# A decoder block whose second MLP product is built from seven products: GpSimd adds the sums for pieces (6,0) and (6,1) ahead of those for (7,0) and (7,1)

## The chip, the cores and the metric

The kernel runs on one core of a Trainium2 chip. The metric is the device time of one execution in microseconds (us); lower is better. Every engine of the core runs its own queue of instructions in order, and engines wait for each other by semaphores.

## The reference: what is computed

One decoder layer on 512 tokens of width 1024, in float32. The part that the change touches is the MLP at the end:

```python
h = rms_norm(x, norm_ffn_pre[l])
f = jnp.square(jax.nn.relu(h @ w_ff1[l])) @ w_ff2[l]     # 1024 -> 4096 -> 1024
x = x + rms_norm(f, norm_ffn_post[l])
```

Before it stands a token mixer (a projection to ten parts, three branches, a gated merge, a projection back), which the change leaves as it is.

## The kernel before

**Float32 from two halves.** Each matrix of weights comes from memory in units of 128x1024 float32 (512 KB). ScalarE rounds a unit to `w_hi` (line 521, `ff_hi`), VectorE writes the rest as `w_lo` (line 765, `ff_lo`), and TensorE makes each product from three: hi by hi, hi by lo, lo by hi (lines 1147 to 1151). `w_hi` and `w_lo` are rings of four buffers, so the unit u is split once TensorE is through with unit u-4.

**The MLP in quarters.** The hidden width of 4096 is cut into four quarters of 1024 (`q`). A quarter is 22 units: 8 of `w_ff1` (24 matmuls each), and then 14 pieces of `w_ff2` (12 matmuls each). The second matmul is made from seven products of half-size blocks instead of eight, as in Strassen's and Winograd's schemes; piece (p,h) is half h of what product p takes from the weights. TensorE's order is

```python
PIECES = ((1, 0), (5, 0), (2, 0), (1, 1), (5, 1), (6, 0), (2, 1), (6, 1),
          (3, 0), (3, 1), (7, 0), (7, 1), (4, 0), (4, 1))
```

The products 6, 7, 4 and 3 are laid on top of an earlier product in the same PSUM bank (`ON_TOP_OF`: 6 on 1, 7 on 6, 4 on 7, 3 on 5). TensorE may start them only when VectorE has added the earlier one to the result (`add_product`, line 1080). For 7 and 4 both halves are used token tile by token tile, so (4,0) and (4,1) are both needed at the start.

**Sums of weights.** Products 5, 6, 4 and 7 need a sum of blocks. It is made by the DMA: GpSimd issues a transfer from memory that adds onto what lies in the buffer (line 505, `add_blocks`). In 5, 6 and 4 the sum grows: (5,h) is loaded by SP into slot 6+h (tile `glu`) and one block is added; when it has been split, a second block is added in place for (6,h); when that has been split, a third for (4,h). The sum for (7,h) is apart: SP loads a block into one of the six slots that the plain loads use in turn (tiles `raw`, `raw_v`, `raw_c`), and GpSimd adds one onto it. In each quarter there are eight such transfers, 32 in all.

**What the queues wait for.** GpSimd waits, for (5,h) and (7,h), for SP's load of the slot (`raw_loaded`), and for (6,h) and (4,h), for the split of the piece that lay in the slot (`w_lo_ready`): (6,0) for the split of (5,0), (6,1) for that of (5,1), (4,0) and (4,1) for those of (6,0) and (6,1). ScalarE waits for the sum (`raw_added`) before `w_hi`. VectorE's order among the pieces (lines 1103 to 1121): for each piece in TensorE's order it waits for the piece to be done, adds finished products, and then splits the piece four further on. So the `w_lo` of (6,0) and of (2,1) stands ahead of the two adds of product 1, on which product 6 waits; and the `w_lo` of (4,1) stands ahead of the first add of product 7, on which product 4 waits. SP (lines 388 to 404) loads the 512 KB units in order, each when the one that was last in its slot has been split.

Of the kernel before, what the change touches and what calls it, by code (L numbers as in the profile page):

```python
# [94 lines left out]
def piece_unit(q, n):  # L95
    return ff_unit(q, KT + n)
# [26 lines left out]
def is_loaded(u):  # L123
    return piece_of(u)[0] not in ADDED or piece_of(u)[0] in LOADED
# [6 lines left out]
def earlier_in_slot(u):  # L131
    return [v for v in range(U_FF, u) if FF_SLOT[v] == FF_SLOT[u]]


def ff_loads(u):
    before = U_FF // RAW if FF_SLOT[u] < RAW else 0
    return 16 * (before + sum(is_loaded(v) for v in earlier_in_slot(u)) + 1)
# [6 lines left out]
def source(u, added=False):  # L144

    q, k = divmod(u - U_FF, PER_QUARTER)
    product, h = piece_of(u)
    if product is None:
        return U_FF + 2 * KT * q + k
    k_half, n_half = (ADDED if added else LOADED)[product]  # L150
    return U_FF + 2 * KT * q + KT + CH * n_half + 2 * k_half + h
# [50 lines left out]
def build(nc, x_d, units_d, cols_d, rows_d, ws_d, bs_d, out_d):  # L202
    with ExitStack() as ctx:
# [210 lines left out]
        def _(pool):  # L414
# [80 lines left out]
            def add_blocks(q, products):  # L495
                for n, (product, h) in enumerate(PIECES):
                    if product not in products:
                        continue
                    u = piece_unit(q, n)
                    slot = FF_SLOT[u]  # L500
                    if is_loaded(u):
                        pool.wait_ge(raw_loaded[slot], ff_loads(u))
                    else:
                        pool.wait_ge(w_lo_ready, earlier_in_slot(u)[-1] + 1)
                    pool.dma_start(slots[slot], units_d[source(u, added=True)],
                                   accum_op=ALU.add).then_inc(raw_added[slot], 16)

            for q in range(QUARTERS):
                add_blocks(q, (5,))
                add_blocks(q, (7,))  # L510
                add_blocks(q, (6,))
                add_blocks(q, (4,))

            for n, c in enumerate(FINAL):
# [247 lines left out]
        def _(dve):  # L762
# [313 lines left out]
            def add_product(q, product, t):  # L1076

                _, bank, (m_half, n_half, sign) = PRODUCTS[product]
                y = by_token[:, 2 * m_half + t, half_of(n_half)]
                nc.vector.tensor_tensor(y, y, ps[:, bank + t, :],  # L1080
                                        ALU.add if sign > 0 else ALU.subtract).then_inc(mlp_sum, 1)
# [343 lines left out]
```

## Time and profile before

| | us |
|---|---|
| median of 3 runs | 999.98 (999.39 to 1000.72) |
| the profiled execution | 999.11 |
| its span in the trace | 997.4 |
| outside the span | 1.7 |

The span is what the views of the trace divide; the profiled execution is 0.87 us under the median. In a row of the timeline stand the start, the time taken, the engine, the line and the tiles; in brackets the idle time of the engine before it and who ended that. "issue" there means that the profile shows no instruction that ended the wait; the landing of a transfer can be behind it. The profile models the end of each matmul: 128x512 ones are shown 0.39 us long but start 0.23 us apart in a full row.

### The profile page before, as it was taken

What the parts mean: (1) busy time and instruction counts of PE and PEld (TensorE: products, weight loads), DVE (VectorE), ACT (ScalarE), POOL (GpSimd) and SP (SyncE); (2) the same over time, 40 slices, a digit from 0 to 9 for tenths busy, and PEclk for the clock granted to TensorE, in tenths of its full rate; (3) what the DMA queues carried; (4) which work ended last, traced back from release to release, by engine and by line L of the source; (5) the groups of instructions that cost most, each with busy time, mean ns of one, the idle gap of its engine ahead of it and who ended that gap; (6) DMA issues with size and microseconds to landing.
All of it is one profiled execution on the core that took longest, in us unless ns stands there. A gap on an engine that the chain in (4) does not pass through costs nothing.

```text
span 997.4 us, 12346 instructions
## 1 busy us (share of the span) xinstructions
PE 969.9 (97%) x4380; PEld 805.7 (81%) x4380; DVE 675.3 (68%) x829; ACT 382.3 (38%) x493; POOL 98.3 (10%) x115
## 2 busy tenths in 40 slices
PE   5999999999999999999999999999899899999996
PEld 4888888888888888888888888898788788878885
DVE  5348889888888988886584443755645574565568
ACT  5333332333333322224463322545335434533543
POOL 3000000000000011114000000121100100110012
PEclk9999999999999999999999999999999999999999
DMA  6323322223223122233226234074845667475472
GB/s 218 118 82 112 106 89 90 100 95 103 95 86 105 64 98 91 84 106 112 100 87 251 93 100 165 23 224 118 205 152 150 132 179 202 113 195 178 118 126 85
DMA packets 34629, 123.35 MB, mean 124 GB/s; under 512 B 4000, under 2 KB 4128, under 8 KB 34592
## 3 DMA queue, kind: packets, MB, share of 16 engines
q1 hardware_dynamic: 28368, 100.84, 29.6%
q0 software_dynamic: 5120, 17.83, 10.5%
q10 hardware_dynamic: 1104, 4.19, 1.1%
q8 instruction: 23, 0.38, 0.1%
q14 instruction: 14, 0.11, 0.0%
HBM read 120.75 MB, written 2.10 MB: 123 GB/s over the span
## 4 chain that ended last, share of the span: by engine, by line
PE 95%; DVE 2%; issue 1%; ACT 1%; DMA 1%; POOL 0%; DVEq 0%; POOLq 0%; ACTq 0%
PE ps L1147 30%; PE ps L1151 30%; PE ps L1149 30%; DVE w_lo L765 1%; PE ps L1190 1%; PE ps L1304 1%; PE ps L1305 1%; PE ps L1303 1%; DVE wide L1080 1%; DMA conf<-x_in 1%; PE ps L1253 0%; PE ps L1254 0%; DVE wide L1093 0%; PE ps L1252 0%; ACT w_hi L521 0%
## 5 line engine op out<-in xcount | busy, mean ns | idle before, releaser
L765 DVE TENSOR_TENSOR w_lo<-raw,w_hi 128x1024 fp32r<-128x1024 f32 x130 | 160.4, 1237 | 115.7 <-ACT w_hi L521 115.4
L1147 PE MATMUL ps<-a_hi,w_hi 128*128 128x512 f32 x576 | 225.4, 391 | 0.0
L1149 PE MATMUL ps<-a_lo,w_hi 128*128 128x512 f32 x576 | 224.2, 389 | 0.0
L1151 PE MATMUL ps<-a_hi,w_lo 128*128 128x512 f32 x576 | 224.1, 389 | 0.0
L521 ACT ACTIVATE w_hi<-raw 128x1024 fp32r<-128x1024 f32 x130 | 137.0, 1056 | 198.5 <-PE ps L1151 135.5
L842 DVE SCALAR_TENSOR_TENSOR conf<-glu,cols,conf (+1 forms) x240 | 186.9, 779 | 27.5 <-DVE conf L842 26.4
L1147 PE MATMUL ps<-b_hi,w_hi 128*128 128x512 f32 x360 | 140.2, 390 | 0.0
L1151 PE MATMUL ps<-b_hi,w_lo 128*128 128x512 f32 x360 | 140.1, 389 | 0.0
L1149 PE MATMUL ps<-b_lo,w_hi 128*128 128x512 f32 x360 | 140.0, 389 | 0.0
L1149 PEld LDWEIGHTS ps<-a_lo,w_hi 128*128 128x128 f32 x576 | 108.2, 188 | 22.7 <-issue 0.5
L1147 PEld LDWEIGHTS ps<-a_hi,w_hi 128*128 128x128 f32 x576 | 108.1, 188 | 22.6 <-DVE w_lo L765 0.2
L1151 PEld LDWEIGHTS ps<-a_hi,w_lo 128*128 128x128 f32 x576 | 108.1, 188 | 22.5
L1147 PE MATMUL ps<-w_hi,set_hi 128*128 128x512 f32 x224 | 89.1, 398 | 8.4 <-DVE wide L1080 8.4
L1149 PE MATMUL ps<-w_lo,set_hi 128*128 128x512 f32 x224 | 88.3, 394 | 0.0
L1151 PE MATMUL ps<-w_hi,set_lo 128*128 128x512 f32 x224 | 88.1, 393 | 0.0
L1147 PEld LDWEIGHTS ps<-b_hi,w_hi 128*128 128x128 f32 x360 | 67.6, 188 | 14.2 <-DVE b_lo L766 0.3
L1151 PEld LDWEIGHTS ps<-b_hi,w_lo 128*128 128x128 f32 x360 | 67.6, 188 | 14.1
L1149 PEld LDWEIGHTS ps<-b_lo,w_hi 128*128 128x128 f32 x360 | 67.6, 188 | 14.0
L1147 PEld LDWEIGHTS ps<-w_hi,set_hi 128*128 128x128 f32 x224 | 42.8, 191 | 19.2 <-DVE w_lo L765 9.8
L765 DVE TENSOR_TENSOR w_lo<-glu,w_hi 128x1024 fp32r<-128x1024 f32 x24 | 29.4, 1223 | 37.9 <-ACT w_hi L521 35.7
L1151 PEld LDWEIGHTS ps<-w_hi,set_lo 128*128 128x128 f32 x224 | 42.8, 191 | 9.2
L1149 PEld LDWEIGHTS ps<-w_lo,set_hi 128*128 128x128 f32 x224 | 42.9, 192 | 8.8
(154 smaller groups left out, 1170.3 us busy)
## 6 DMA issues: line engine op xcount, KB each, us to landing
raw<-units_in SPq DMA_DIRECT2D x134, 512.0 KB, 3.3
glu<-units_in POOLq DMA_DIRECT2D x24, 512.0 KB, 6.1
raw_v<-units_in SPq DMA_DIRECT2D x22, 512.0 KB, 4.3
raw_c<-units_in SPq DMA_DIRECT2D x20, 512.0 KB, 4.1
glu<-units_in SPq DMA_DIRECT2D x8, 512.0 KB, 5.3
conf<-x_in SPq DMA_DIRECT2D x4, 512.0 KB, 8.0
glu<-rows_in ACTq DMA_DIRECT2D x4, 512.0 KB, 10.7
conf<-x_in ACTq DMA_DIRECT2D x1, 2048.0 KB, 9.0
```

What stands on the lines that cost most here:

```text
L521: return nc.scalar.activation(dst, src, ACT.Copy, scale=scale)
L765: return nc.vector.tensor_tensor(dst, src, hi, ALU.subtract)
L842: nc.vector.scalar_tensor_tensor(out=conf[:, tile, :], in0=glu[:, tile, k:k + SEQ], scalar=cols[:, tile, COL_CONF + k:COL_CONF + k + 1], i ...
L1080: nc.vector.tensor_tensor(y, y, ps[:, bank + t, :], ALU.add if sign > 0 else ALU.subtract).then_inc(mlp_sum, 1)
L1147: nc.tensor.matmul(ps[:, bank, :], left_hi, right_hi, start=first, stop=False, skip_group_check=on_top)
L1149: nc.tensor.matmul(ps[:, bank, :], left_hi, right_lo, start=False, stop=False, skip_group_check=on_top)
L1151: return nc.tensor.matmul(ps[:, bank, :], left_lo, right_hi, start=False, stop=final, skip_group_check=on_top)
L1190: mm = nc.tensor.transpose(ps[:, banks + g, k * P:(k + 1) * P], by_token[:, c, at:at + P], ident[:, :])
L1303: nc.tensor.matmul(out, w_hi[:, u.ring, w], b_hi[:, k, tokens], start=k == 0, stop=False)
L1304: nc.tensor.matmul(out, w_hi[:, u.ring, w], b_lo[:, k, tokens], start=False, stop=False)
L1305: mm = nc.tensor.matmul(out, w_lo[:, u.ring, w], b_hi[:, k, tokens], start=False, stop=k == KT - 1)
```

## The change

In `add_blocks`' calling loop the order of two calls is exchanged. GpSimd's order in a quarter was 5, 7, 6, 4 and is 5, 6, 7, 4, with h = 0 and 1 of each. The same 32 transfers are issued, with the same waits; no other engine's queue changes.

```diff
             for q in range(QUARTERS):
                 add_blocks(q, (5,))
+                add_blocks(q, (6,))
                 add_blocks(q, (7,))
-                add_blocks(q, (6,))
                 add_blocks(q, (4,))
```

GpSimd's queue in the first quarter and at the start of the second. `glu` is the tile of the growing sums; those that wait for `raw_loaded6` and `raw_loaded7` are (5,0) and (5,1); those on `raw_v` and `raw` are (7,0) and (7,1); those that wait for `w_lo_ready` are of 6 and 4:

```order
 L505 DMA glu<-units_in 128x1024 [waits raw_loaded6]
 L505 DMA glu<-units_in 128x1024 [waits raw_loaded7]
+L505 DMA glu<-units_in 128x1024 [waits w_lo_ready] x2
 L505 DMA raw_v<-units_in 128x1024 [waits raw_loaded2]
 L505 DMA raw_v<-units_in 128x1024 [waits raw_loaded3]
-L505 DMA glu<-units_in 128x1024 [waits w_lo_ready] x4
+L505 DMA glu<-units_in 128x1024 [waits w_lo_ready] x2
 L505 DMA glu<-units_in 128x1024 [waits raw_loaded6]
```

Four transfers of the growing sums stood in a row behind the two of product 7; now the two for product 6 stand ahead of them, and the two for product 4 behind.

GpSimd's queue in the last quarter, up to the reduction that follows it:

```order
 L505 DMA glu<-units_in 128x1024 [waits raw_loaded7]
+L505 DMA glu<-units_in 128x1024 [waits w_lo_ready] x2
 L505 DMA raw_v<-units_in 128x1024 [waits raw_loaded2]
 L505 DMA raw_v<-units_in 128x1024 [waits raw_loaded3]
-L505 DMA glu<-units_in 128x1024 [waits w_lo_ready] x4
+L505 DMA glu<-units_in 128x1024 [waits w_lo_ready] x2
 L432 TENSOR_SCALAR meansq<-sumsq 128x1 [waits sumsq_ready]
```

The same exchange; the queue still ends with the two transfers for product 4.

## Rows read from the trace of the kernel before

**Rows 1.** The page: span, and the chain that ended last, by engine.
```profile
span 997.4 us, 12346 instructions
...
PE 95%; DVE 2%; issue 1%; ACT 1%; DMA 1%; POOL 0%; DVEq 0%; POOLq 0%; ACTq 0%
```

**Rows 2.** Timeline, start and us taken: matmuls after the idle stretches, one a quarter.
```profile
710.39 0.76 PE L1147 MATMUL ps<-w_hi,set_hi 128*128 128x512 f32 x1 [2.65 <-DVE wide L1080]
...
796.55 0.47 PE L1147 MATMUL ps<-w_hi,set_hi 128*128 128x512 f32 x1 [2.88 <-DVE wide L1080]
...
880.68 0.74 PE L1147 MATMUL ps<-w_hi,set_hi 128*128 128x512 f32 x1 [2.27 <-DVE wide L1080]
...
964.56 0.47 PE L1147 MATMUL ps<-w_hi,set_hi 128*128 128x512 f32 x1 [0.40 <-DVE wide L1080]
```

**Rows 3.** Stretches: us, busy time (x instructions) by engine, PE clock, DMA share, GB/s.
```profile
710.40:713.50 3.10, 3.10 (x8) 2.44 (x9) 2.87 (x5) 1.59 (x2) 0.86 (x1) 0.51 0.91 174
796.50:799.60 3.10, 3.05 (x14) 2.55 (x14) 2.80 (x4) 1.72 (x2) 0.78 (x1) 1.00 1.00 188
880.70:884.20 3.50, 3.50 (x9) 2.76 (x10) 2.85 (x5) 2.00 (x2) 0.86 (x1) 0.51 0.97 199
```

**Rows 4.** Timeline of VectorE, first quarter.
```profile
684.94 1.23 DVE L765 TENSOR_TENSOR w_lo<-glu,w_hi 128x1024 fp32r<-128x1024 f32 x1 [3.50 <-ACT w_hi L521]
...
701.60 1.22 DVE L765 TENSOR_TENSOR w_lo<-glu,w_hi 128x1024 fp32r<-128x1024 f32 x1
707.28 1.23 DVE L765 TENSOR_TENSOR w_lo<-glu,w_hi 128x1024 fp32r<-128x1024 f32 x1 [4.46 <-ACT w_hi L521]
708.43 1.22 DVE L765 TENSOR_TENSOR w_lo<-raw_c,w_hi 128x1024 fp32r<-128x1024 f32 x1
709.56 1.27 DVE L1080 TENSOR_TENSOR wide<-wide,ps 128x512 f32<-128x512 f32 x2
```

**Rows 5.** Timeline of ScalarE, first quarter: splits of (6,0), (6,1), (4,0), (4,1).
```profile
706.12 1.06 ACT L521 ACTIVATE w_hi<-glu 128x1024 fp32r<-128x1024 f32 x1 [4.74 <-issue]
...
709.98 1.06 ACT L521 ACTIVATE w_hi<-glu 128x1024 fp32r<-128x1024 f32 x1 [1.85 <-issue]
...
723.07 1.06 ACT L521 ACTIVATE w_hi<-glu 128x1024 fp32r<-128x1024 f32 x1 [1.66 <-PE ps L1151]
725.79 1.06 ACT L521 ACTIVATE w_hi<-glu 128x1024 fp32r<-128x1024 f32 x1 [1.66 <-PE ps L1151]
```

**Rows 6.** Timeline of GpSimd: issues for (7,0), (7,1), (6,0), (6,1), (4,0).
```profile
685.08 0.86 POOL L505 DMA_DIRECT2D raw_v<-units_in  x1 [14.55 <-DMA raw_v<-units_in]
695.87 0.86 POOL L505 DMA_DIRECT2D raw_v<-units_in  x1 [9.94 <-DMA raw_v<-units_in]
696.41 1.21 POOL L505 DMA_DIRECT2D glu<-units_in  x1
703.12 0.86 POOL L505 DMA_DIRECT2D glu<-units_in  x1 [5.50 <-DVE w_lo L765]
708.80 0.86 POOL L505 DMA_DIRECT2D glu<-units_in  x1 [4.83 <-DVE w_lo L765]
```

**Rows 7.** Line 505 in 695:704, 781:790, 866:874, 952:960: (7,1), (6,0), (6,1).
```profile
DMA to landing us min/median/max: 6.5/6.8/9.6
...
L505 POOL DMA_DIRECT2D glu<-units_in x2: 863/1040/1218, 782.4 to 789.1; - x2
...
DMA to landing us min/median/max: 5.3/7.1/9.8
...
L505 POOL DMA_DIRECT2D glu<-units_in x2: 863/1040/1218, 867.1 to 873.8; - x2
...
DMA to landing us min/median/max: 5.2/6.8/9.3
...
DMA to landing us min/median/max: 5.4/5.6/7.4
```

**Rows 8.** Timeline of SP's queue: the load behind (7,1) and the next one.
```profile
697.07 12.92 SPq L404 DMA_DIRECT2D raw_c<-units_in  x2
```

## Prediction, made before the changed kernel was timed

> **What bounds the kernel now.** The page comes first. TensorE's matmuls are 95% of the chain that ended last [rows 1], so only a stretch in which TensorE stands still, or runs slower, can be saved. The timeline of TensorE over the MLP has one such stretch in every quarter, always ahead of the first matmul of piece (6,0) [rows 2]. The idle time there is counted from the modelled end of the matmul before, which is shown 0.39 us long where the next may start after 0.23. So the start is late by the idle time + 0.39 - 0.23: 2.81, 3.04, 2.43 and 0.56 us, together 8.84 us. Behind two of the four the granted clock is 0.51, the lower of its two levels, 1.2 GHz where full speed is 2.4: for 3.1 us after the first stall and 3.5 us after the third. Behind the second, the longest, it is 1.00 [rows 3]. A stretch of 3.1 us at 0.51 does the work of 1.6 us, so 1.5 us are lost, and 1.7 in the other: 3.2 us. Stalls and slow clock cost **12.1 us** in this execution.
>
> The reader should now follow one stall backwards, the first. TensorE was released at 710.39 by VectorE's add of product 1, which started at 709.56. That add stood in VectorE's order behind two splits, at 707.28 and 708.43, and the first of them, the `w_lo` of (6,0), had waited 4.46 us for ScalarE [rows 4]. ScalarE had been idle for 4.74 us and started the `w_hi` of (6,0) at 706.12, with no instruction that released it [rows 5]: what came was the sum. GpSimd had issued the transfer for (6,0) at 696.41, right behind that for (7,1) at 695.87 [rows 6], and it took 9.6 us to land, the largest of the three in that stretch [rows 7], so until 706.0. The same shape stands in the next two quarters (9.8 and 9.3 us), and a milder one in the last (7.4 us), which has a stall of 0.56 us only.
>
> When could it have been issued? The slot was free when the `w_lo` of (5,0) was done, at 684.94 + 1.23 = 686.2 [rows 4]. GpSimd stood until 695.87 at the wait for SP's load of (7,1) [rows 6], with (6,0) queued behind. This is what the exchange takes away: 10 us of waiting for another piece's load.
>
> **What the change takes away.** (6,0) is issued at 686.2 and lands some 6 us later, near 692. ScalarE needs it at about 701.5, so 9 us are to spare and the late sum is gone in all four quarters. What is late next at that place? VectorE's two splits then end by about 705.2 and the first add of product 1 by 705.8, before TensorE comes to (6,0) at 710.39 - 2.81 = 707.58. Its cover there is 1 us or more. So all 12.1 us go, if nothing new comes. Issuing costs GpSimd the same 0.86 us each in either order, and nobody waits for GpSimd itself there.
>
> **What the change adds.** The transfers move in GpSimd's queue past one wait. (6,1) may be issued only when (5,1) has been split, 701.60 + 1.22 = 702.8 [rows 4], and that moment is set by TensorE's pace, so its issue stays at 703.12 [rows 6]. (7,0) and (7,1), which used to go out at 685.08 and 695.87 in an emptier time, now stand behind it and go at about 703.7 and 704.2. (4,0), ready since the early split of (6,0) at about 704, goes at 704.8, and (4,1) when (6,1) has been split, near 711. **Five transfers in a row** replace a spread of them, and the last is the one to follow.
>
> The first of a row took 6.5, 5.3, 5.2 and 5.4 us [rows 7]; I take 5.4, so (6,1) lands at 708.5. The step from one landing to the next in such a row comes from the same rows, with issues 0.54 us apart for (7,1) and (6,0), and 6.7 us for (6,0) and (6,1) (703.12 - 696.41 [rows 6]; 782.4 to 789.1 and 867.1 to 873.8 [rows 7]).
> - With a plain load of SP's between them, as the one issued at 697.07 [rows 8]: 9.6 - 6.5 + 0.5 = 3.6, then 9.8 - 5.3 + 0.5 = 5.0 and 9.3 - 5.2 + 0.5 = 4.6. Mean 4.4 us.
> - Without one: 6.8 - 9.6 + 6.7 = 3.9, then 4.0 and 4.2. Mean 4.0 us. In the last quarter, where SP has no load left, 7.4 - 5.4 + 0.5 = 2.5 us.
>
> From (6,1) to (4,1) are four steps. SP issues loads when (2,1), (3,0) and (3,1) have been split, now near 705, 713.5 and 715, so three of the steps have a load between. They give 3 x 4.4 + 4.0 = 17.2 us, and (4,1) lands at 725.7. The bounds are 3 x 3.6 + 2.5 = 13.3 (721.8) and 3 x 5.0 + 4.2 = 19.2 (727.7). No row shows five in a queue, so both ends are kept; I take the means, as the busy quarters are the nearest.
>
> What does it meet? From the landing of a sum to TensorE's start behind the add, the first stall shows 0.1 us to ScalarE, 1.16 to VectorE's split, 1.15 to the next in its row and 0.83 from the start of the add to the matmul [rows 2, 4, 5], 3.2 us in all. The same order stands before product 4: split of (4,1), add of product 7, matmul. So TensorE starts (4,0) at 728.9. Without delay it would come there at 707.58 + 7 pieces x 2.72 (the step of 723.07 to 725.79 in [rows 5]) = 726.6. It is **2.3 us late**. In the kernel before, ScalarE took these two sums without waiting for them, released by TensorE [rows 5], so this stall is wholly new. (7,0) and (7,1) are wanted later in their turn (first matmul at 707.58 + 5 x 2.72 = 721.2) and land at about 713 and 717; (6,1) leaves 2 us of cover. These cost nothing, nor do SP's loads that come later, since the next quarter's units have 20 us and more.
>
> In the last quarter no load stands between: 959.6 + 5.4 + 4 x 2.5 = 975.0, and it is wanted by 964.0 + 19.0 - 3.2 = 979.8. It costs nothing, or 1.2 us at 4.0 us a step.
>
> **The sum.** Three new stalls of 2.3 us are 6.9 us. For the clock: the shortest old stall that it fell behind was 2.43 us and one of 3.04 us had none, so I charge one drop of 1.6 us for the three. Added: 8.5 us. Removed: 12.1 us. Net -3.6 us on 999.11 us gives 995.5 us, and on the median, which lies 0.87 us higher, **996.4 us**.
>
> A page speaks on the price of a transfer. The trace has 5.2 to 6.5 us for the first of a row of sums and steps of 2.5 to 5.0 us behind it [rows 7]. The Trainium skill ("DMA: Bandwidth & Descriptors", section "Anatomy of one DMA — SWDGE (gpsimd) path") fits a transfer issued by GpSimd as 2.0 us plus its bytes at 436 GB/s. By that, an estimate, 512 KB would take 3.2 us with steps of 1.2 us, the row of five would be over by about 713, and the time would be that of the first rival. The trace doesn't agree, at less than half the speed; these transfers add, which the fit doesn't treat.
>
> **The rivals.**
> - *The gain stays whole.* If the steps are short, 3.6 us or less with a load between, or if SP's loads fall behind the sums instead of between them (four steps of 3.9 us end at 724.1, half a microsecond or so late), (4,1) comes by 723.4 and nothing is late. For it: 2.5 us in the last quarter. Against it: all three busy quarters have 3.9 us or more where no load is between. Time: 999.98 - 12.1 = 987.9 us.
> - *The crowd costs more than the wait did (slower).* The place is VectorE's split of (4,1) ahead of the add of product 7. With steps at the upper bound (4,1) lands at 727.7, TensorE starts at 730.9, 4.3 us late, and with the clock falling each time the three quarters cost 3 x (4.3 + 1.6) = 17.7 us: +5.6 us, 1005.6 us. It decides from a landing of about 725.8, where stall and clock drop together are 4.0 us a quarter (727.4 with no drop). My 725.7 is close to that. For it: the DMA engines are at 0.91 to 1.00 of their time around there already [rows 3], and two transfers more come in. Against it: each such step was only seen once or twice in a row.
> - *The two cancel.* A landing near 726 with one or two drops, or a sum for (6,1) that lands 1.5 us later than I take and holds (6,1) as (6,0) was held: within 2 us of 1000.
> - *The change doesn't do what it says.* GpSimd would have to be held by something else at 686. No row has that, since it sat idle until the load of (7,1); it has no chance of its own.
>
> **How the numbers follow.** Forecast case (2 to 3 us late in three quarters): 0.42, of which 0.32 is faster by more than 0.2% and 0.10 within. Whole gain: 0.14. Cancelled: 0.15. Slower: 0.29. A difference of 0.2%, 2 us, is about what a measurement of this kernel can tell from none. That makes faster 0.46, same 0.25, slower 0.29. The range goes from the whole gain to just under the bound of the crowd, 987.8 to 1005.0 us. The likeliest case by itself, with a landing of (4,1) between 725 and 726.3, spans some 993 to 999 us.
>
> **What would show it.** Right: no idle time before (6,0) at 707.6, and the row for (6,0) landing in 5 to 6 us; GpSimd's issues at 703.1, 703.7, 704.2 and 704.8; a new idle stretch before the first matmul of (4,0), with ScalarE waiting for `glu` ahead of it, in three quarters and not in the last. Wrong: no stall there (steps too long in my sum), stalls of 4 us or more (too short), or an idle stretch before (6,1) or (7,0) (another transfer of the row is the late one).

## The result and the profile after

The changed kernel takes **987.08 us** (median of 4 runs, 986.88 to 987.60). The kernel before, with a fourth run of 1003.16 us beside the three of the table, has a median of 1000.35 us. The ratio is 0.9864, with a 95% interval of 0.9843 to 0.9884: about 13 us faster. The prediction said 996.4 us in a range of 987.8 to 1005.0. The direction was right and the size was not: the time lies 0.7 us outside the range, at the first rival ("the gain stays whole", 987.9 us).

The page of the profile after shows the same lines as in [rows 1]. Behind it stands the view of waits over the MLP, for TensorE (us in total, times, longest):

```profile
span 985.1 us, 12346 instructions
...
PE 97%; DVE 1%; DMA 1%; issue 0%; ACT 0%; POOL 0%; POOLq 0%; DVEq 0%; ACTq 0%
```

```profile
PE ps L1147 <- DVE wide L1080: 0.2, 1, 0.2
```

The span is 12.3 us shorter. In the MLP TensorE waits once, for 0.2 us between 970 and 975 us, near the end of the kernel; the four stretches of [rows 2] are gone, and nothing stands in their place. GpSimd's timeline in the first quarter, which answers to [rows 6]:

```profile
686.50 0.86 POOL L505 DMA_DIRECT2D glu<-units_in  x1 [16.15 <-DVE w_lo L765]
703.16 0.86 POOL L505 DMA_DIRECT2D glu<-units_in  x1 [15.80 <-DVE w_lo L765]
703.70 2.10 POOL L505 DMA_DIRECT2D raw_v<-units_in  x2
704.78 1.91 POOL L505 DMA_DIRECT2D glu<-units_in  x1
711.17 0.87 POOL L505 DMA_DIRECT2D glu<-units_in  x1 [4.49 <-DVE w_lo L765]
```

(6,0) goes out at 686.5 and (6,1), (7,0), (7,1), (4,0) in a row from 703.16 on, 0.54 us apart; (4,1) follows at 711.17. That is the row of five of the prediction, at its times to within 0.3 us. How long each took is in the view of line 505. The first answer has (6,1), (7,0) and (7,1), the second (7,0), (7,1) and (4,0), the third (4,1) alone:

```profile
DMA to landing us min/median/max: 5.3/9.1/11.1
...
DMA to landing us min/median/max: 9.1/11.1/13.5
...
DMA to landing us min/median/max: 10.9/10.9/10.9
```

They land at 708.5, 712.8, 715.3, 718.3 and 722.1. The four steps are 4.3, 2.5, 3.0 and 3.8 us, 13.6 in all where the prediction had 17.2. The timelines of ScalarE, VectorE and TensorE show what the last one meets:

```profile
708.56 1.06 ACT L521 ACTIVATE w_hi<-glu 128x1024 fp32r<-128x1024 f32 x1 [5.04 <-DMA glu<-units_in]
...
722.19 1.06 ACT L521 ACTIVATE w_hi<-glu 128x1024 fp32r<-128x1024 f32 x1 [2.36 <-DMA glu<-units_in]
```

```profile
723.28 1.23 DVE L765 TENSOR_TENSOR w_lo<-glu,w_hi 128x1024 fp32r<-128x1024 f32 x1 [0.59 <-ACT w_hi L521]
724.43 0.68 DVE L1080 TENSOR_TENSOR wide<-wide,ps 128x512 f32<-128x512 f32 x1
```

```profile
726.65 0.39 PE L1147 MATMUL ps<-w_hi,set_hi 128*128 128x512 f32 x1
```

ScalarE does wait for the sum now, 2.36 us before (4,1), as the prediction said it would (in [rows 5] TensorE had released it). But the chain behind it ends with the add at 724.43 + 0.68 = 725.1, and TensorE comes to (4,0) at 726.65, without an idle moment. The crowd is there; in this quarter it lands 1.5 us before it would cost anything.

The other quarters are not alike. In the second the margin is 1.5 us again, and in the last there is no wait for a sum: TensorE released ScalarE before both pieces of product 4. In the third, (4,1) lands latest. Timelines of ScalarE and VectorE:

```profile
886.45 1.06 ACT L521 ACTIVATE w_hi<-glu 128x1024 fp32r<-128x1024 f32 x1 [2.71 <-DMA glu<-units_in]
```

```profile
887.54 1.23 DVE L765 TENSOR_TENSOR w_lo<-glu,w_hi 128x1024 fp32r<-128x1024 f32 x1 [1.28 <-ACT w_hi L521]
888.68 0.68 DVE L1080 TENSOR_TENSOR wide<-wide,ps 128x512 f32<-128x512 f32 x1
```

The add ends at 889.36 and TensorE starts (4,0) at 889.85, so only 0.5 us were left there.

### The profile page after: what moved, and what is told of

The parts are those of the page before. It is cut to its first block, busy times and chain, and to the rows that moved or that the text cites. A ratio compares the mean times of both kernels' runs of the same rounds, so it can differ in the third digit from the quotient of the medians.

```text
span 985.1 us, 12346 instructions
## 1 busy us (share of the span) xinstructions
PE 965.7 (98%) x4380; PEld 803.9 (82%) x4380; DVE 674.5 (68%) x829; ACT 382.4 (39%) x493; POOL 98.6 (10%) x115
## 3 DMA queue, kind: packets, MB, share of 16 engines
q0 software_dynamic: 5120, 17.83, 10.2%
## 4 chain that ended last, share of the span: by engine, by line
PE 97%; DVE 1%; DMA 1%; issue 0%; ACT 0%; POOL 0%; POOLq 0%; DVEq 0%; ACTq 0%
PE ps L1147 31%; PE ps L1151 31%; PE ps L1149 31%; PE ps L1190 1%; PE ps L1304 1%; PE ps L1305 1%; PE ps L1303 1%; DMA conf<-x_in 1%; DVE wide L1080 0%; PE ps L1253 0%; PE ps L1254 0%; DVE wide L1093 0%; PE ps L1252 0%; DVE a_lo L765 0%; ACT ps L546 0%
## 5 line engine op out<-in xcount | busy, mean ns | idle before, releaser
L505 POOL DMA_DIRECT2D glu<-units_in x24 | 25.1, 1047 | 270.4 <-DVE w_lo L765 154.5
```

The source lines that it names most:

```text
L505: pool.dma_start(slots[slot], units_d[source(u, added=True)], accum_op=ALU.add).then_inc(raw_added[slot], 16)
```

## The experiments

Two questions were open. What in the old order made (6,0) late: its late issue, or what stood before it in the transfer queue? And why did the row of five run faster than the steps in [rows 7]? Each kernel was timed beside the kernel before on the same chip, and the ratios are to that. Line numbers move by a few lines from kernel to kernel.

**The transfer for (6,0) alone goes ahead.**

```diff
-                add_blocks(q, (5,))
-                add_blocks(q, (7,))
-                add_blocks(q, (6,))
-                add_blocks(q, (4,))
+                for piece in ((5, 0), (5, 1), (6, 0), (7, 0), (7, 1), (6, 1), (4, 0), (4, 1)):
+                    add_piece(q, piece)
```

(`add_piece` is `add_blocks` for one piece.)

> Only the transfer for (6,0) goes ahead of those of product 7; (6,1) stays behind them: order (5,0) (5,1) (6,0) (7,0) (7,1) (6,1) (4,0) (4,1). Theory A (the whole old stall hangs on (6,0) alone): the stall before (6,0) is gone in all quarters, (7,0) is issued near 687 and (7,1) near 696, there is no row of five, and the time is that of the change, 987 us within 1. Theory B (part of the gain of the change comes from (6,1) going earlier): some idle time is left before (6,0) or (6,1), and the time lies 2 us or more above 987.

Measured: 987.17 us (986.53 to 987.27), ratio 0.9875 (0.9844 to 0.9905). GpSimd's timeline:

```profile
686.89 0.86 POOL L505 DMA_DIRECT2D glu<-units_in  x1 [16.06 <-DVE w_lo L763]
687.42 1.21 POOL L505 DMA_DIRECT2D raw_v<-units_in  x1
696.43 0.85 POOL L505 DMA_DIRECT2D raw_v<-units_in  x1 [7.80 <-DMA raw_v<-units_in]
```

Theory A holds. The whole gain hangs on the one transfer for (6,0), and that (6,1) went ahead too brought nothing. Here (7,0) and (7,1) go out at 687.4 and 696.4, so this order has the gain without the crowd.

**(6,0) ahead of (7,1), but issued no earlier.**

```diff
+                for piece in ((5, 0), (5, 1), (7, 0), (6, 0), (7, 1), (6, 1), (4, 0), (4, 1)):
+                    if piece == (6, 0):
+                        u = piece_unit(q, PIECES.index((7, 1)))
+                        pool.wait_ge(raw_loaded[FF_SLOT[u]], ff_loads(u))
+                    add_piece(q, piece)
```

> The transfer for (6,0) stands ahead of that for (7,1), but GpSimd still waits for the load of (7,1) before it issues it, so that it goes out at about 695.9 as before and only its place in the transfer queue differs. Queue theory (what cost time was the 3.6 to 5 us behind (7,1)'s transfer): (6,0) lands 5.2 to 6.5 us after its issue, at 701.1 to 702.4; ScalarE wants it at 701.4, so TensorE is late by 0.5 us at most, and the time is 987 to 989 us. Late-issue theory (what cost time was the 10 us wait for the load): the stalls stay, and the time is 995 us or more.

Measured: 987.10 us (987.02 to 987.28), ratio 0.9876 (0.9846 to 0.9906). Timelines of GpSimd and ScalarE:

```profile
696.30 0.86 POOL L505 DMA_DIRECT2D glu<-units_in  x1 [9.96 <-DMA raw_v<-units_in]
696.83 1.20 POOL L505 DMA_DIRECT2D raw_v<-units_in  x1
```

```profile
702.89 1.06 ACT L522 ACTIVATE w_hi<-glu 128x1024 fp32r<-128x1024 f32 x1 [1.04 <-PE ps L1152]
```

The issue is where it was before (696.3, and 696.41 in [rows 6]); only the neighbour in the queue changed places, and the whole gain is there. The sum lands 6.5 us after its issue, at 702.8, a little later than I gave, and ScalarE's split starts at 702.9 instead of 706.1. (The row names TensorE as what released it, but the landing is what came last.) That is still 1.04 us after ScalarE was free, and VectorE's slack covers it. So the queue theory holds. The 10 us for which GpSimd was held did no harm by themselves, though they used up the slack; the 3.2 us that (6,0) lost by standing behind the transfer for (7,1) did the harm.

**The two sums for product 7 last: the slower rival, made to happen.**

```diff
+                for piece in ((5, 0), (5, 1), (6, 0), (6, 1), (4, 0), (4, 1), (7, 0), (7, 1)):
+                    add_piece(q, piece)
```

> GpSimd's order in a quarter is 5, 6, 4, 7: the two sums for product 7 go out last, after (4,1) at about 711.2, though TensorE wants product 7 from 721.2. With short steps (2.5 to 3.8 us, as in the row of five of the changed kernel) (7,0) lands near 719.5 to 720 and (7,1) near 722.5 to 723.5; from a landing to TensorE it is 2.4 us, so TensorE starts (7,0) late by 0.7 to 3 us in the three busy quarters: 989 to 998 us, with the stall before the first matmul of (7,0). With the steps that the prediction took (4.0 to 4.4 us) (7,0) lands near 722 or later and the stall is 4 us or more a quarter, 1000 us or more.

Measured: 1007.23 us (1005.21 to 1010.21), ratio 1.0078 (1.0054 to 1.0103): slower than the kernel before. Timelines of ScalarE and of TensorE, first quarter:

```profile
720.57 1.06 ACT L519 ACTIVATE w_hi<-raw_v 128x1024 fp32r<-128x1024 f32 x1 [9.02 <-DMA raw_v<-units_in]
724.38 1.06 ACT L519 ACTIVATE w_hi<-raw_v 128x1024 fp32r<-128x1024 f32 x1 [2.75 <-DMA raw_v<-units_in]
```

```profile
723.54 0.50 PE L1145 MATMUL ps<-w_hi,set_hi 128*128 128x512 f32 x1 [2.29 <-DVE wide L1078]
...
726.75 0.50 PE L1145 MATMUL ps<-w_hi,set_hi 128*128 128x512 f32 x1 [1.55 <-DVE w_lo L763]
```

The sums landed at 720.5 and 724.3. The first is within a microsecond of what short steps gave and the second later, with plain loads between again. The time missed my range mainly because I had counted one stall a quarter. There are two, one for each half: 2.45 and 1.7 us late here, and 13.5 us over the four quarters. The chain from the first landing to TensorE was also 3.0 us (720.5 to 723.54) where I had 2.4. The rest is one more wait of 2.23 us, at 991.05, and a clock that fell in the third quarter and at the end (0.50 from 899.2 to 903.0). That an order of these eight transfers can lose more than the old stall cost is shown.

**No plain loads in the row.**

```diff
             for u in range(U_FF, UNITS):
...
+                if u >= ff_unit(1, 0) and (u - U_FF) % PER_QUARTER == 1:
+                    v = piece_unit((u - U_FF) // PER_QUARTER - 1, PIECES.index((4, 1)))
+                    sp.wait_ge(raw_added[FF_SLOT[v]], sums_in_slot(v))
                 sp.dma_start(slots[slot], units_d[source(u)]).then_inc(raw_loaded[slot], 16)
```

> The changed order, but SP holds its loads from the second w_ff1 unit of the next quarter on until the sum for (4,1) has landed, so no plain load stands in or beside the row of five. Theory A (plain loads share the DMA engines and cost the row what they move, about 1.5 us each): the steps between landings fall to 2.5 us and (4,1), issued at 711.2, lands at about 718.5 to 719 in place of 722.1. Theory B (the row keeps its own pace, and plain loads only wait): (4,1) lands at 721 to 722 as before. The time stays at 987 us under both, if the held loads still come in time.

Measured: 986.70 us (986.37 to 987.12), ratio 0.9871 (0.9841 to 0.9902). Issues, and the times to landing: the first answer has (6,1) and (7,0), the second (7,0), (7,1) and (4,0), the third (4,1):

```profile
703.43 0.86 POOL L508 DMA_DIRECT2D glu<-units_in  x1 [15.80 <-DVE w_lo L766]
703.97 2.10 POOL L508 DMA_DIRECT2D raw_v<-units_in  x2
705.05 1.91 POOL L508 DMA_DIRECT2D glu<-units_in  x1
711.42 0.87 POOL L508 DMA_DIRECT2D glu<-units_in  x1 [4.47 <-DVE w_lo L766]
```

```profile
DMA to landing us min/median/max: 5.3/6.3/7.3
...
DMA to landing us min/median/max: 7.3/9.3/11.2
...
DMA to landing us min/median/max: 7.5/7.5/7.5
```

Landings at 708.7, 711.3, 713.8, 716.3 and 718.9: steps of 2.5 to 2.6 us. Theory A holds: in this quarter a queued sum takes 2.5 us, and the loads had added 3.4 us over the four steps (10.9 against 7.5 for (4,1)). But the changed kernel had five loads issued in that row, at 705.2, 713.2, 714.4, 716.7 and 719.0, so one cost it about 0.7 us on average, not the 1.5 us that I had put. In the next two quarters the four steps together took 11.4 us each, not 10.2, because single steps were 2.7 to 3.6 us long with no load there; why is open. The changed kernel had 13.7 and 14.7. So the loads' share is 2.3 to 3.4 us a row.

**The old order without the load in the row.**

```diff
+                if u >= ff_unit(1, 0) and (u - U_FF) % PER_QUARTER == 0:
+                    v = piece_unit((u - U_FF) // PER_QUARTER - 1, PIECES.index((6, 1)))
+                    sp.wait_ge(raw_added[FF_SLOT[v]], sums_in_slot(v))
                 sp.dma_start(slots[slot], units_d[source(u)]).then_inc(raw_loaded[slot], 16)
```

> The order of before (5, 7, 6, 4), but SP holds its load of the next quarter's first w_ff1 unit, which went out at 697.1 between the transfers for (7,1) and (6,0), until the sum for (6,1) has landed. Theory A (steps in GpSimd's row are 2.5 us and the load made the rest): (6,0) lands at about 704.9 in place of 706.0 (7.9 in place of 9.6 us after its issue; 9.8 and 9.3 become 7.9 too), (6,1) at 708.5 in place of 709.9, and each of the three large stalls shrinks by 1.1 to 2.3 us: 993 to 997 us. Theory B (a transfer behind another in the row costs 3.6 to 5 us by itself): landings and stalls as before, 999 us.

Measured: 992.48 us (990.42 to 996.14), ratio 0.9932 (0.9913 to 0.9952). Line 508 in the first quarter, (7,1), (6,0) and (6,1) as in [rows 7], then (6,1) alone; and the matmuls of [rows 2]:

```profile
DMA to landing us min/median/max: 5.2/5.9/7.8
...
DMA to landing us min/median/max: 5.2/5.2/5.2
```

```profile
708.75 0.47 PE L1150 MATMUL ps<-w_hi,set_hi 128*128 128x512 f32 x1 [0.87 <-DVE wide L1083]
...
792.04 0.47 PE L1150 MATMUL ps<-w_hi,set_hi 128*128 128x512 f32 x1 [1.40 <-DVE wide L1083]
...
875.21 0.47 PE L1150 MATMUL ps<-w_hi,set_hi 128*128 128x512 f32 x1 [1.32 <-DVE wide L1083]
...
957.37 0.47 PE L1150 MATMUL ps<-w_hi,set_hi 128*128 128x512 f32 x1 [0.31 <-DVE wide L1083]
```

(6,0) lands 7.8 us after its issue in place of 9.6, and (6,1) 5.2 in place of 6.8. So the step from (6,0) to (6,1), which the prediction took as one without a load, was not the pace of a queue: with the load held back, (6,1) takes no longer than a transfer alone. In the next two quarters (6,0) takes 8.3 and 8.2 us, so the step behind (7,1) is 2.4 us in the first quarter and 3.5 and 3.4 in those, and the load had added 1.2 to 1.5 us to each. (It is issued at 697.07, 0.7 us behind (6,0) at 696.41, so it ran beside the two sums rather than between them.) The starts are late by 1.03, 1.56, 1.48 and 0.47 us (idle time + 0.39 - 0.23), together 4.5 us where it had been 8.8, and the clock did not fall in this execution. The load beside the two sums had thus made about half of the late starts and, with the clock, over half of the old cost (7.2 us of the median); the rest needs only the sum for (7,1) ahead. The median is slightly below the 993 us that I gave, and the third start shrank by 0.95 us, less than the 1.1 that I gave.

**(4,1) issued late: the price of the new chain.**

```diff
+                for piece in ((5, 0), (5, 1), (6, 0), (6, 1), (7, 0), (7, 1), (4, 0), (4, 1)):
+                    if piece == (4, 1):
+                        pool.wait_ge(w_lo_ready, piece_unit(q, PIECES.index((7, 1))) + 1)
+                    add_piece(q, piece)
```

> The changed order, but GpSimd issues the sum for (4,1) only when (7,1) has been split, at about 719.3 in place of 711.2, so it lands at 724.7 to 726.8 in place of 722.1. If the chain of the prediction holds (3.2 us from that landing over split, next in VectorE's row, add of product 7, to TensorE; wanted by 723.4), TensorE starts (4,0) 1.3 to 3.4 us late in the three busy quarters and about 1.3 us in the last: 992 to 1001 us, the upper part where the clock falls behind the stalls. If (4,1)'s split is not on that chain (TensorE could go on with another tile), the time stays within 1 us of 987 and there is no idle stretch before (4,0).

Measured: 1004.51 us (1001.39 to 1008.07), ratio 1.0044 (1.0026 to 1.0062). Timelines of ScalarE, VectorE and TensorE, and the stretches behind the four stalls, as in [rows 3]:

```profile
726.66 1.06 ACT L521 ACTIVATE w_hi<-glu 128x1024 fp32r<-128x1024 f32 x1 [6.60 <-DMA glu<-units_in]
```

```profile
727.75 1.23 DVE L765 TENSOR_TENSOR w_lo<-glu,w_hi 128x1024 fp32r<-128x1024 f32 x1 [4.83 <-ACT w_hi L521]
728.89 1.47 DVE L1080 TENSOR_TENSOR wide<-wide,ps 128x512 f32<-128x512 f32 x2
```

```profile
729.63 0.79 PE L1147 MATMUL ps<-w_hi,set_hi 128*128 128x512 f32 x1 [2.59 <-DVE wide L1080]
```

```profile
729.60:732.70 3.10, 3.07 (x7) 2.48 (x8) 2.96 (x3) 0.01 (x1) 0.00 (x0) 0.51 0.08 17
816.00:819.00 3.00, 3.00 (x13) 2.48 (x14) 2.96 (x3) 0.00 (x0) 0.00 (x0) 1.00 0.10 19
901.10:906.80 5.70, 5.67 (x14) 4.47 (x15) 3.10 (x4) 0.01 (x1) 0.00 (x0) 0.51 0.47 130
988.90:992.10 3.20, 3.16 (x8) 2.50 (x9) 3.14 (x5) 1.25 (x3) 1.06 (x2) 0.51 0.30 112
```

The chain is as predicted: the landing at 726.6, split, next in VectorE's row, add, TensorE at 729.63, which is 3.0 us from the landing where the prediction had 3.2. The start is 2.75 us late, and 3.2 to 3.5 us in the other three quarters. The total is over my range for two reasons. The last quarter is 3.5 us late, not 1.3, and the clock fell behind three of the four stalls, once for 5.7 us.

**The changed kernel again.**

> The changed kernel itself beside the two others, on the same chip: 987 us within 1, no idle stretch of TensorE in the quarters, and the five landings of the row at the steps seen before (4.3, 2.5, 3.0 and 3.8 us within half a microsecond).

Measured: 986.89 us (986.47 to 987.37), ratio 0.9867 (0.9835 to 0.9898). It stands as expected beside the others. No stall stands in the quarters, and the four steps of the first row are 4.3, 2.6, 3.0 and 3.8 us. No order tried is faster than it beyond the spread of the runs. With no stall left there, moving these transfers has nothing more to give.

## Why the prediction was wrong in size

- **What the change removes: right.** 12.1 us of late starts and slow clock, all before (6,0), was the sum; the span fell by 12.3 us, and the four stretches are gone. (6,0) landed near 692 and the cover there was enough, as worked out.
- **Why (6,0) was late: half right.** The prediction named "10 us of waiting for another piece's load" as what the exchange takes away. The kernel that kept this wait, and only put (6,0) ahead of (7,1) in the queue, has the whole gain. The harm was in the queue: a step of 2.4 to 3.5 us behind (7,1)'s sum, and 1.2 to 1.5 us more from the plain load beside it. Issuing (6,0) early is one way out of that, and standing ahead of (7,1) is enough.
- **The row of five and its times of issue: right**, and so was the chain behind (4,1), 3.0 us measured for 3.2.
- **The step between landings: the term that was mis-sized.** It was taken at 4.4 us with a load between and 4.0 us without, so 17.2 us for four steps; measured were 13.6, 13.7 and 14.7 us in the three busy quarters. Both figures came from the distance between two landings in the old order, and neither was the pace of a full queue. The 4.0 us stood between (6,0) and (6,1). But (6,1) had been issued only 3 us before (6,0) landed, so that distance held (6,1)'s own time from issue to landing (5.2 us when the load was held back), and an effect of the load. The 4.4 us stood between the first two of a row with a load beside them, and for that step it was right (4.3, 4.3 and 4.7 us measured); the later steps of the first quarter, with loads beside them too, took 2.5, 3.0 and 3.8. The pace stood in the one row that I kept as a bound only, 2.5 us in the last quarter of [rows 7]. The kernel without loads has it in the first quarter and in most steps of the others, 10.2 to 11.4 us for four. The loads add 2.3 to 3.4 us to that, for five of them; the prediction had counted three.
- **What followed.** (4,1) landed at 722.1 instead of 725.7, before the 723.4 at which it would begin to cost, and the 8.5 us of new stalls and clock were not there. In the third quarter it was close: 14.7 us of steps left 0.5 us. That no quarter paid anything is thus partly luck. The lower bound of the landing, 721.8, was in the text; the chance of 0.14 for that case was too small, and the range ended at it with nothing to spare.
- **The slower rival** was a real mechanism in the wrong place: the kernel that delays (4,1) starts 2.75 us late and more in every quarter, and the one that puts product 7 last 2.45 and 1.7 us late in the first. The changed kernel stands 1.5 us from such a stall in the first two quarters and 0.5 us in the third.

## What to carry to other kernels

When transfers are queued one behind another, take the pace of the queue from landings of transfers that were all issued well before, and not from pairs of which the second was issued just before the first landed; that distance is mostly the second one's own time from issue to landing. Before blaming a wait for a late buffer, ask what stands in front of it in the transfer queue. Put the transfer that is wanted first ahead even where the other is ready too. And a change that removes waits in an in-order queue can make a crowd somewhere later: find the last of the crowd, and compare its landing, in every repetition of the pattern, with the moment at which its consumer's whole chain begins to be late.

## What the runs showed of the hardware

- Adding transfers of 512 KB that are queued one behind another land 2.5 to 2.6 us apart with SP's loads held back (first quarter; single steps of 2.7 to 3.6 us in the others), though one alone takes 5.2 to 5.5 us from issue to landing. The five loads of SP's that fall beside them in the changed kernel add 2.3 to 3.4 us to the row, and wait themselves: they take this long, where the page of the profile gives 3.3 us as the median of SP's loads into `raw`:

```profile
DMA to landing us min/median/max: 6.4/7.7/8.5
```

- The clock behind a stall of TensorE is not told by the length of the stall. In the kernel with (4,1) late the granted clock was 0.51 behind late starts of 2.75, 3.4 and 3.5 us, and 1.00 behind one of 3.2 us; in the kernel before, 0.51 behind 2.81 and 2.43 us and 1.00 behind 3.04 us; with product 7 last, 1.00 behind 2.45 us. What decides it was not settled.
- Kernels without such stalls repeat better. The changed kernel's second set of runs spans 986.47 to 987.37 us, while the runs of the kernel before in the same comparison span 997.06 to 1002.87 us. The granted clock of each run, as a mean over it, goes with that: 0.997 in the fastest of those runs of the kernel before and 0.991 in the slowest, and 0.998 to 0.999 in the four of the changed kernel. So the spread is one of the clock: 0.6% of 1000 us is 6 us, as much as lies between the two. That it falls behind different stalls from run to run is argued, since only one execution of each kernel has a trace.
